# A bias line stored earlier in the load queue, x loaded first, squares ahead of the line copy, and nine products of zeros ahead of the first square sums

## The chip, the cores and the metric

The kernel runs on one core of one Trainium2 chip. The metric is the time of one execution on the device in microseconds (us), as the median of repeated runs. The core has five engines that run side by side: TensorE (PE in the profile, its weight loads PEld), VectorE (DVE), ScalarE (ACT), GpSimd (POOL) and SyncE (SP), which here issues almost all DMA transfers. They are ordered by semaphores alone.

## The reference, cut to what matters

The reference is two transformer-like blocks on 256 tokens of width 1024. What the change touches is the very beginning of the first block:

```python
# first layer: pool mixer, then a gated feed-forward
x = x + pool_mixer(rmsnorm(x, norm_mixer[0]), pool_w[0], pool_scale[0])
x = x + swiglu(rmsnorm(x, norm_ffn[0]), w_gate_up[0], w_down[0])

def rmsnorm(x, g):
    return x * rsqrt(mean(x * x) + EPS) * g
# pool_mixer: window sums of 2, 4, 8, 16 tokens / counts - h, then a 256x256 product per group
# attention, much later: scores + rel_bias[bucket(distance)] per head
# second block: mod = silu(c) @ ada_w + ada_b   (a 1024 x 6144 matrix)
```

After it come attention with a relative bias, a second feed-forward, and a second block with attention, an RWKV branch and 64 experts.

## The kernel before

All work is written out by hand, one program per engine. Tokens lie along the free dimension, features along the partitions, in eight chunks of 128; `x`, `h` and `sq` are 128 x 8 x 256. Weights stream through a ring of 11 slots of 1536 KB each; SP issues the loads in a fixed order, and what it issues is worked off in that order.

SP's order at the start (L505 to L527) is: the 33 x 512 selector, the 33 x 24 relative bias `relw`, the vectors `vecs`, `x`, the inverse counts, two slots of the modulation matrix (`load_ada(0)`, `load_ada(1)`), the pool weights, `load_ada(2)`, `load_ada(3)`, the first feed-forward slot (`load(0)`, a `ws` transfer), then a wait for `line_copied`, the constants `con`, the store `bias_line<-scr`, and the further `ws` slots. The store writes one 512-wide line per head (24 heads) to DRAM, each repeated 32 times, so that the attention can later read it back in shifted form (`bias1`, read by POOL some hundred microseconds later).

The line itself is one small product: PE multiplies `relw` with the selector (L799), ACT copies the result out of PSUM into `line_sb` (L1426, `line_copied`). ACT then squares x (`norm_squares(0)`, L1366, four instructions), PE sums the squares with a matrix of ones (`norm_sum(0)`, L693), and ACT takes the root into `rt` (L1369). DVE makes the normalized `hp` (L1753, L1755), the window sums (L1870 to L1873) and four groups of pool inputs (L1878, L1879), each group signalled by `pool_d`. PE meanwhile does the first three quarters of the modulation product (`modulation(0, 0, 6)`, L792), which wants the `ada` slots 0, 1 and 2, and stands ahead of the pool products (L811) in its program; the last quarter and `norm_sum(1)` come behind them.

ACT waits for all four `pool_d` and for slot 0 of `ws`, and copies that slot's gate and up part into `gu_hi` (L1376). DVE's program at this place is the function `first_start`:

```python
                pool_residual(0)
                pool_residual(1)
                split()                      # slot_lo <- slot 0 - gu_hi, L1759: waits for ACT's gu_hi
                dve.wait_ge(line_stored, 16)
                h_lo_pair(0)                 # L1768
                pool_residual(2)             # L1885
                h_lo_pair(1)
                pool_residual(3)
                h_lo_pair(2)
                h_lo_pair(3)
                add_modulation(0)
```

`line_stored` must be waited for before the feed-forward because `act_hi`, which DVE writes in it, lies over `line_sb`. The residuals 2 and 3 behind it release ACT's last two pairs of squares, these the last products of `norm_sum(1)`, and these the feed-forward's four clearing products (L699) and its long row of products in three parts (L715 to L717).

Of the kernel before, what the change touches and what calls it, by code (L numbers as in the profile page):

```python
# [12 lines left out]
ACT = mybir.ActivationFunctionType  # L13
# [4 lines left out]
P = 128  # L18
T = 256
# [18 lines left out]
SHIFTS = 32  # L38
# [110 lines left out]
def build(nc, xT, vec, consts, selector, inv_count, pool_w, ws, ada, rel, lora, router, router_bias, experts, final_row, out):  # L149
# [4 lines left out]
    with ExitStack() as ctx:  # L154
# [347 lines left out]

        @block.sync
        def _(sp):
            sp.dma_start(sel_sb[0:BUCKETS + 1, :], selector).then_inc(sel_loaded, 16)  # L505
            sp.dma_start(relw[:], rel).then_inc(sel_loaded, 16)
            sp.dma_start(vecs[:], vec).then_inc(vec_loaded, 16)
            sp.dma_start(x[:], xT).then_inc(x_loaded, 16)
            sp.dma_start(icnt, inv_count).then_inc(pool_loaded, 16)

            def load(n):
# [2 lines left out]
            def load_ada(a):  # L514
                p = ADA_PLACE[a]
                sp.dma_start(ring[:, p * SLOT:(p + 1) * SLOT], ada[a]).then_inc(landed[p], 16)

            load_ada(0)
            load_ada(1)
            sp.dma_start(poolw, pool_w).then_inc(pool_loaded, 16)  # L520
            load_ada(2)
            load_ada(3)
            load(0)
            sp.wait_ge(line_copied, 1)
            heads = HEADS_1 + HEADS_2
            sp.dma_start(con[:], consts).then_inc(const_loaded, 16)
            sp.dma_start(bias_line, line_sb[0:heads, :].unsqueeze(1).broadcast_to([heads, SHIFTS, 2 * T])).then_inc(line_stored, 16)  # L527

            def load_after(n, signal, value):
                sp.wait_ge(signal, value)  # L530
# [153 lines left out]
        def _(pe):  # L684
# [3 lines left out]
            def norm_sum(k, bank=B[6], weights=lambda c: ones[:]):  # L688

                for g in range(4):  # L690
                    pe.wait_ge(sq_ready, SQ_BASE[k] + g + 1)
                    for c in (2 * g, 2 * g + 1):
                        mm = nc.tensor.matmul(bank[:, 0:T], weights(c), sq[:, c, :], start=(c == 0), stop=(c == KC - 1))  # L693
                mm.then_inc(ss_ready, 1)
# [86 lines left out]
            def modulation(g, c0, c1):  # L781
# [5 lines left out]
                for c in range(c0, c1):  # L787
# [6 lines left out]
                    if (c + 1) * chunk // SLOT > first:  # L794
                        mm.then_inc(ada_used, 1)

            pe.wait_ge(ones_ready, 1)
            pe.wait_ge(sel_loaded, 32)
            nc.tensor.matmul(B[7][0:HEADS_1 + HEADS_2, :], relw[:], sel_sb[0:BUCKETS + 1, :], start=True, stop=True).then_inc(pe_step, 1)  # L799


            norm_sum(0)
            pe.wait_ge(csil_ready, 2)
            pe.wait_ge(line_copied, 1)
            modulation(0, 0, 6)
# [541 lines left out]
        def _(act):  # L1347
            def load_table(func):

                nc.scalar.activation(small[:, 60:61], eps, func)  # L1350
# [68 lines left out]
                return exponentials, outputs, turned_weights  # L1419

            act.wait_ge(ones_ready, 1)
            act.wait_ge(vec_loaded, 16)
            nc.scalar.activation(csig, vecs[:, VEC["c"][0]:VEC["c"][1]], ACT.Sigmoid).then_inc(csil_ready, 1)
            load_table(ACT.Sqrt)
            act.wait_ge(pe_step, 1)
            nc.scalar.activation(line_sb[0:HEADS_1 + HEADS_2, :], B[7][0:HEADS_1 + HEADS_2, :], ACT.Copy).then_inc(line_copied, 1)  # L1426
            norm_squares(0)

            act.wait_ge(pool_d, 4)
            ffn_start(S_FFN1)  # L1430
# [311 lines left out]
        def _(dve):  # L1742
# [129 lines left out]
            then(nc.vector.tensor_tensor(pw_b[:, 4:, 7:W], pw_c[:, 4:, 7:W], pw_c[:, 4:, 3:W - 4], ALU.add))  # L1872
            then(nc.vector.tensor_tensor(pw_c[:, 6:, 15:W], pw_b[:, 6:, 15:W], pw_b[:, 6:, 7:W - 8], ALU.add))  # L1873
            dve.wait_ge(pool_loaded, 32)
            for g in range(4):
                win = (pw_b, pw_c)[g % 2][:, 2 * g:2 * g + 2, PAD:]
                hg = h[:, 2 * g:2 * g + 2, :]
                then(nc.vector.tensor_tensor(hg, win, icnt[:, g:g + 1, :].broadcast_to([P, 2, T]), ALU.mult))  # L1878
                nc.vector.tensor_tensor(hg, hg, hp[:, 2 * g:2 * g + 2, PAD:], ALU.subtract).then_inc(pool_d, 1)  # L1879
# [576 lines left out]
```

## Time and profile before

| | |
|---|---|
| three runs | 1401.15, 1398.17, 1400.96 us, median 1400.96 |
| the profiled execution | 1400.87 us, its span 1399.2 us |
| PE busy | 1330.1 us, 95% of the span |
| DVE, ACT, POOL busy | 678.1, 510.9, 197.9 us |
| mean granted TensorE clock | 0.986 |
| chain that ended last | PE 82%, DVE 8%, ACT 3%, DMA 3% |

The span runs from the first instruction to the last. The table says that PE works nearly all the time; what is left to gain without taking work from PE lies where PE waits, and the change is at the start of the program.

### The profile page before, as it was taken

To read this page: it belongs to the slowest core of one execution; us is meant where nothing else is said; L and a number is where in the kernel's file an instruction comes from. 1 tells how busy PE (TensorE), PEld (TensorE's weight loads), DVE (VectorE), ACT (ScalarE), POOL (GpSimd) and SP (SyncE) were. 2 spreads that over 40 slices of the span, in tenths; PEclk is the share of its full clock that TensorE was granted. 3 is DMA by queue.
4 is the path that set the end of the run, shared out by engine and by line. 5 is a ranking of instruction groups with operands and counts; after the bars stand their busy time and mean duration, and the time that the engine had idled before them with its cause. 6 is when DMAs were issued, how large, how long until landed. Compare 5 with 4: busy or idle time off the path is not lost.

```text
span 1399.2 us, 24627 instructions
## 1 busy us (share of the span) xinstructions
PE 1330.1 (95%) x10580; PEld 1013.9 (72%) x10580; DVE 678.1 (48%) x1075; ACT 510.9 (37%) x829; POOL 197.9 (14%) x96
## 2 busy tenths in 40 slices
PE   5899999999999999999997889999999999999997
PEld 3899999988899999799895789744444444444433
DVE  6665665666666665788985443511121112212113
ACT  2433433556533333467454442222222222222212
POOL 0000000000000000376781663000000000000002
PEclk9999999999999999999999999999999999999999
DMA  9965455745455336452316035349999999999994
GB/s 370 408 271 185 176 185 217 302 130 215 168 182 188 148 123 231 193 215 96 138 46 271 3 118 225 122 193 423 423 426 426 423 428 426 422 428 424 422 426 174
DMA packets 37507, 363.43 MB, mean 260 GB/s; under 512 B 5027, under 2 KB 6179, under 8 KB 8740
## 3 DMA queue, kind: packets, MB, share of 16 engines
q1 hardware_dynamic: 36692, 359.56, 63.8%
q0 software_dynamic: 720, 2.46, 0.9%
q8 instruction: 77, 1.26, 0.4%
q14 instruction: 18, 0.15, 0.0%
HBM read 359.32 MB, written 2.69 MB: 259 GB/s over the span
## 4 chain that ended last, share of the span: by engine, by line
PE 82%; DVE 8%; ACT 3%; DMA 3%; POOL 2%; issue 1%; SPq 0%; DVEq 0%; POOLq 0%; ACTq 0%
PE banks L1289 16%; PE banks L715 13%; PE banks L717 13%; PE banks L716 13%; PE banks L1314 8%; PE banks L1240 4%; PE banks L1249 4%; DMA bias_line<-scr 2%; POOL slot_lo L627 2%; PE banks L693 1%; PE banks L704 1%; PE banks L1255 1%; DMA scr<-bias_line 1%; PE banks L1063 1%; DVE ring L2077 1%
## 5 line engine op out<-in xcount | busy, mean ns | idle before, releaser
L715 PE MATMUL banks<-h_hi,gu_hi 128*128 128x256 f32 x704 | 199.5, 283 | 0.0
L717 PE MATMUL banks<-h_hi,slot_lo 128*128 128x256 f32 x704 | 199.2, 283 | 0.0
L716 PE MATMUL banks<-h_lo,gu_hi 128*128 128x256 f32 x704 | 199.2, 283 | 0.0
L717 PE MATMUL banks<-slot_lo,slot_lo 128*128 128x256 f32 x480 | 136.3, 284 | 0.0
L715 PEld LDWEIGHTS banks<-h_hi,gu_hi 128*128 128x128 f32 x704 | 135.2, 192 | 0.7 <-DVE slot_lo L1759 0.5
L716 PEld LDWEIGHTS banks<-h_lo,gu_hi 128*128 128x128 f32 x704 | 135.2, 192 | 0.0
L717 PEld LDWEIGHTS banks<-h_hi,slot_lo 128*128 128x128 f32 x704 | 135.2, 192 | 0.0
L2313 DVE TENSOR_TENSOR out_lo<-banks,out_hi 128x512 fp32r<-128x512 f32 x62 | 42.9, 692 | 185.0 <-ACT out_hi L1701 185.0
L1314 PE MATMUL banks<-ring,scr 128*64 128x512 f32 x512 | 116.9, 598 | 1.9 <-ACT scr L1695 1.9
L1289 PE MATMUL banks<-ring,scr 128*64 128x512 f32 x512 | 112.6, 592 | 0.0
L1289 PE MATMUL banks<-ring 128*64 128x512 f32 x512 | 112.6, 592 | 0.0
L1759 DVE TENSOR_TENSOR slot_lo<-ring,gu_hi 128x2048 fp32r<-128x2048 f32 x44 | 100.7, 2292 | 14.4 <-ACT gu_hi L1380 14.0
L1392 ACT ACTIVATE scr<-scr 128x256 f32<-128x256 f32 x44 | 18.4, 418 | 236.1 <-DVE scr L1788 236.1
L2291 DVE TENSOR_TENSOR scr<-banks,scr 128x256 f32<-128x256 f32 x32 | 13.6, 425 | 184.1 <-ACT scr L1688 184.1
L715 PE MATMUL banks<-act_hi,down_hi 128*128 128x256 f32 x352 | 99.9, 284 | 2.6 <-DVE slot_lo L1759 2.6
L716 PE MATMUL banks<-act_lo,down_hi 128*128 128x256 f32 x352 | 99.6, 283 | 0.0
L717 PE MATMUL banks<-act_hi,slot_lo 128*128 128x256 f32 x352 | 99.6, 283 | 0.0
L627 POOL TENSOR_TENSOR slot_lo<-ring,win_hi 128x1024 fp32r<-128x1024 f32 x20 | 48.4, 2426 | 314.4 <-ACT win_hi L1508 314.4
L717 PEld LDWEIGHTS banks<-slot_lo,slot_lo 128*128 128x128 f32 x480 | 92.2, 192 | 0.0
L1289 PEld LDWEIGHTS banks<-ring,scr 128*64 128x64 f32 x512 | 36.7, 137 | 73.3 <-issue 73.3
L1289 PEld LDWEIGHTS banks<-ring 128*64 128x64 f32 x512 | 36.8, 137 | 73.0 <-issue 73.0
L1688 ACT ACTIVATE scr<-banks 128x256 f32<-128x256 f32 x32 | 12.3, 385 | 208.5 <-PE banks L1289 208.5
(420 smaller groups left out, 2985.3 us busy)
## 6 DMA issues: line engine op xcount, KB each, us to landing
ring<-experts SPq DMA_DIRECT2D x64, 2048.0 KB, 10.9
ring<-ws SPq DMA_DIRECT2D x77, 1536.0 KB, 7.2
ring<-experts SPq DMA_DIRECT2D x64, 1024.0 KB, 11.0
ring<-ada SPq DMA_DIRECT2D x16, 1536.0 KB, 7.0
ring<-experts SPq DMA_DIRECT2D x1, 3072.0 KB, 10.1
scr<-bias_line POOLq DMA_DIRECT2D x4, 512.0 KB, 8.0
bias_line<-scr SPq DMA_DIRECT2D x1, 1536.0 KB
x<-xT SPq DMA_DIRECT2D x1, 1024.0 KB, 5.3
```

The costliest lines, as they stand in the source:

```text
L627: nc.gpsimd.tensor_tensor(dst, src, hi.bitcast(F32), ALU.subtract).then_inc(win_w_lo, 1)
L693: mm = nc.tensor.matmul(bank[:, 0:T], weights(c), sq[:, c, :], start=(c == 0), stop=(c == KC - 1))
L715: nc.tensor.matmul(out, hi, move_hi, start=start, stop=False, skip_group_check=True)
L716: nc.tensor.matmul(out, hi, move_lo, start=False, stop=False, skip_group_check=True)
L717: return nc.tensor.matmul(out, lo, move_hi, start=False, stop=stop, skip_group_check=True)
L1240: mm = nc.tensor.matmul(bank, tok[:, tb, step * P:(step + 1) * P], pick[buf][:, tb, :], start=(n == 0 and tb == 0), stop=(n == 1 and tb == ...
L1249: mm = nc.tensor.matmul(B[2 * tb + half], spread[k % 2][:, tb * P:(tb + 1) * P], part[:, half * 512:(half + 1) * 512], start=False, stop=F ...
L1289: mm = nc.tensor.matmul(B[4][CAP * j:CAP * (j + 1), :], gathered_h[o][:, c, at:at + CAP], unit(u)[:, c * 512:(c + 1) * 512], start=(c == 0 ...
L1314: mm = nc.tensor.matmul(B[6 + half][CAP * j:CAP * (j + 1), :], act_pt[:, f, CAP * j:CAP * (j + 1)], unit(u)[:, lo:lo + 512], start=(f == 0 ...
L1392: nc.scalar.activation(gated[:, s % 2, :], gated[:, s % 2, :], ACT.Silu).then_inc(sig_ready, 1)
L1759: nc.vector.tensor_tensor(slot_lo[PLACE[base + s]][:, lo:to], slot(base + s)[:, lo:to], hi.bitcast(F32), ALU.subtract).then_inc(signal, 1)
L2313: ins = nc.vector.tensor_tensor(out_lo[part], B[6 + half], out_hi[part].bitcast(F32), ALU.subtract)
```

## The change

Five edits, all in the first part of the program. SP issues `x` and `vecs` ahead of the selector and `relw`; the store of the bias line stands, with its wait, right behind the pool weights, ahead of `load_ada(2)`, `load_ada(3)` and `load(0)`. PE runs nine products of zeros (128 x 512, bf16) as soon as `ones_ready` is there, then `norm_sum(0)`, and the product of the bias line only behind that. ACT loads the sigmoid table by a small instruction before the vectors are there, and copies the line only behind `norm_squares(0)`. DVE waits for that product (`pe_step`) before it writes `h`, since `h` lies over the selector.

```diff
@@ block.sync
+            sp.dma_start(x[:], xT).then_inc(x_loaded, 16)
+            sp.dma_start(vecs[:], vec).then_inc(vec_loaded, 16)
             sp.dma_start(sel_sb[0:BUCKETS + 1, :], selector).then_inc(sel_loaded, 16)
             sp.dma_start(relw[:], rel).then_inc(sel_loaded, 16)
-            sp.dma_start(vecs[:], vec).then_inc(vec_loaded, 16)
-            sp.dma_start(x[:], xT).then_inc(x_loaded, 16)
             sp.dma_start(icnt, inv_count).then_inc(pool_loaded, 16)
...
             sp.dma_start(poolw, pool_w).then_inc(pool_loaded, 16)
+            sp.wait_ge(line_copied, 1)
+            heads = HEADS_1 + HEADS_2
+            sp.dma_start(bias_line, line_sb[0:heads, :].unsqueeze(1).broadcast_to([heads, SHIFTS, 2 * T])).then_inc(line_stored, 16)
             load_ada(2)
             load_ada(3)
             load(0)
-            sp.wait_ge(line_copied, 1)
-            heads = HEADS_1 + HEADS_2
             sp.dma_start(con[:], consts).then_inc(const_loaded, 16)
-            sp.dma_start(bias_line, line_sb[0:heads, :].unsqueeze(1).broadcast_to([heads, SHIFTS, 2 * T])).then_inc(line_stored, 16)
@@ block.tensor
+            def keep_clock(n):
+
+                for _ in range(n):
+                    nc.tensor.matmul(B[5], zeros[:, 0:P], zeros[:], start=True, stop=True, skip_group_check=True)
+
             pe.wait_ge(ones_ready, 1)
+            keep_clock(9)
+            norm_sum(0)
             pe.wait_ge(sel_loaded, 32)
             nc.tensor.matmul(B[7][0:HEADS_1 + HEADS_2, :], relw[:], sel_sb[0:BUCKETS + 1, :], start=True, stop=True).then_inc(pe_step, 1)
-
-
-            norm_sum(0)
@@ block.scalar
             act.wait_ge(ones_ready, 1)
+            nc.scalar.activation(small[:, 61:62], eps, ACT.Sigmoid)
             act.wait_ge(vec_loaded, 16)
             nc.scalar.activation(csig, vecs[:, VEC["c"][0]:VEC["c"][1]], ACT.Sigmoid).then_inc(csil_ready, 1)
             load_table(ACT.Sqrt)
+            norm_squares(0)
             act.wait_ge(pe_step, 1)
             nc.scalar.activation(line_sb[0:HEADS_1 + HEADS_2, :], B[7][0:HEADS_1 + HEADS_2, :], ACT.Copy).then_inc(line_copied, 1)
-            norm_squares(0)
@@ block.vector
             dve.wait_ge(pool_loaded, 32)
+            dve.wait_ge(pe_step, 1)
             for g in range(4):
```

On SP the two orders stand against each other like this, from the inverse counts on (one piece of the difference; the slots `ring<-ada` and `ring<-ws` are 1536 KB each):

```order
 L509 DMA scr<-inv_count 128x1024
 L516 DMA ring<-ada 128x3072 x2
 L520 DMA scr<-pool_w 128x2048
+L523 DMA bias_line<-scr 768x1x512
 L516 DMA ring<-ada 128x3072 x2
 L512 DMA ring<-ws 128x3072
-L526 DMA con<-consts 128x1505
-L527 DMA bias_line<-scr 768x1x512
+L527 DMA con<-consts 128x1505
 L512 DMA ring<-ws 128x3072 x25
```

The store moved ahead of two `ada` slots and the first `ws` slot, which together are three slots of 1536 KB.

On ACT the order before, from the sigmoid's table to the first copy of a weight slot:

```order
L1423 ACT_TABLE_LOAD
L1423 ACTIVATE small<-vecs 128x8
L1350 ACT_TABLE_LOAD
L1350 ACTIVATE small<-small 128x1
L1426 ACTIVATE scr<-banks 24x512
L1366 ACTIVATE scr<-x 128x512 x4
L1369 ACTIVATE rt<-banks,small 128x256
L1376 ACTIVATE gu_hi_51<-ring 128x2048
```

And of the change (its line numbers are four to six higher):

```order
L1426 ACT_TABLE_LOAD
L1426 ACTIVATE small<-small 128x1
L1428 ACTIVATE small<-vecs 128x8
L1354 ACT_TABLE_LOAD
L1354 ACTIVATE small<-small 128x1
L1370 ACTIVATE scr<-x 128x512 x4
L1373 ACTIVATE rt<-banks,small 128x256
L1432 ACTIVATE scr<-banks 24x512
L1380 ACTIVATE gu_hi_51<-ring 128x2048
```

The copy of the line (`scr<-banks 24x512`) moved from ahead of the squares to behind the root, and one small instruction with the sigmoid's table stands in front.

On PE, the start of the program (one piece of the difference; the store of the line hangs on L799, now L806, by way of ACT's copy):

```order
-L799 MATMUL banks<-scr,relw 24x512
+L800 MATMUL banks<-zeros 128x512 x9
 L693 MATMUL banks<-scr,ones 128x256 x8
+L806 MATMUL banks<-scr,relw 24x512
 L792 MATMUL banks<-ring,small 32x384 x24
-L811 MATMUL banks<-scr 128x256 x16
+L815 MATMUL banks<-scr 128x256 x16
```

The product of the line moved behind the square sums; the modulation (L792) still stands ahead of the pool products (L811, now L815), whose own place is the same.

## Rows read from the trace of the kernel before

**Rows 1.** The page: span, chain that ended last; the windows view after 46.1 us.

```profile
span 1399.2 us, 24627 instructions
...
PE 82%; DVE 8%; ACT 3%; DMA 3%; POOL 2%; issue 1%; SPq 0%; DVEq 0%; POOLq 0%; ACTq 0%
...
46.10:1399.20 1353.10, 1302.52 (x10448) 997.59 (x10446) 650.85 (x1027) 496.84 (x805) 197.66 (x92) 0.99 0.64 256
```

**Rows 2.** Timeline of DVE: start, duration, line, shape, idle time before and releaser.

```profile
32.78 2.29 DVE L1759 TENSOR_TENSOR slot_lo<-ring,gu_hi 128x2048 fp32r<-128x2048 f32 x1 [0.41 <-ACT gu_hi L1376]
38.75 0.88 DVE L1768 SCALAR_TENSOR_TENSOR h_lo<-x,vecs,h_hi 128x256 fp32r<-128x256 f32 x2 [3.67 <-DMA bias_line<-scr]
39.55 0.87 DVE L1885 SCALAR_TENSOR_TENSOR x<-banks,vecs,x 128x256 f32<-128x256 f32 x2
...
41.12 0.87 DVE L1885 SCALAR_TENSOR_TENSOR x<-banks,vecs,x 128x256 f32<-128x256 f32 x2
```

**Rows 3.** Timeline of PE, 3 to 47 us.

```profile
3.13 1.87 PE L799 MATMUL banks<-scr,relw 33*24 33x512 f32 x2 [3.13 <-DMA relw<-rel]
8.14 5.29 PE L693 MATMUL banks<-scr,ones 128*128 128x256 f32 x16 [3.15 <-ACT scr L1366]
...
22.29 2.79 PE L792 MATMUL banks<-ring,small 128*32 128x384 f32 x16 [4.68 <-DMA ring<-ada]
26.97 7.14 PE L811 MATMUL banks<-scr 128*128 128x256 f32 x32 [1.89 <-DVE scr L1879]
34.05 1.50 PE L792 MATMUL banks<-ring,small 128*32 128x384 f32 x16
...
41.93 3.67 PE L693 MATMUL banks<-scr,ones 128*128 128x256 f32 x8 [4.46 <-ACT scr L1366]
45.40 1.08 PE L699 MATMUL banks<-zeros 128*128 128x512 bf16 x4
46.12 0.47 PE L715 MATMUL banks<-h_hi,gu_hi 128*128 128x256 f32 x1
46.43 0.28 PE L716 MATMUL banks<-h_lo,gu_hi 128*128 128x256 f32 x1
```

**Rows 4.** Timeline of ACT, 5 to 43 us.

```profile
5.26 1.28 ACT L1350 ACT_TABLE_LOAD   x1
...
6.67 0.57 ACT L1426 ACTIVATE scr<-banks 24x512 f32<-24x512 f32 x1
7.46 2.19 ACT L1366 ACTIVATE scr<-x 128x512 f32<-128x512 f32 x4 [0.22 <-DMA x<-xT]
...
30.84 1.91 ACT L1376 ACTIVATE gu_hi<-ring 128x2048 fp32r<-128x2048 f32 x1 [16.89 <-DVE scr L1879]
...
42.84 0.61 ACT L1366 ACTIVATE scr<-x 128x512 f32<-128x512 f32 x1
```

**Rows 5.** Timeline of SP, the DMA issues.

```profile
0.88 0.44 SPq L505 DMA_DIRECT2D scr<-selector  x1
...
2.13 0.43 SPq L508 DMA_DIRECT2D x<-xT  x1
...
4.33 0.45 SPq L520 DMA_DIRECT2D scr<-pool_w  x1
4.82 1.08 SPq L516 DMA_DIRECT2D ring<-ada  x2
5.94 0.49 SPq L512 DMA_DIRECT2D ring<-ws  x1
7.26 0.33 SPq L526 DMA_DIRECT2D con<-consts  x1
7.63 0.93 SPq L527 DMA_DIRECT2D bias_line<-scr  x1
```

**Rows 6.** Issues in narrow windows: KB each, us from issue to landing.

```profile
x<-xT SPq DMA_DIRECT2D x1, 1024.0 KB, 5.3
scr<-pool_w SPq DMA_DIRECT2D x1, 1024.0 KB, 14.2
ring<-ada SPq DMA_DIRECT2D x1, 1536.0 KB, 17.4
ring<-ws SPq DMA_DIRECT2D x1, 1536.0 KB, 23.7
con<-consts SPq DMA_DIRECT2D x1, 752.5 KB, 24.6
```

**Rows 7.** Timeline and issue row of the first `ws` behind the store.

```profile
8.62 19.31 SPq L512 DMA_DIRECT2D ring<-ws  x1
...
ring<-ws SPq DMA_DIRECT2D x1, 1536.0 KB, 35.9
```

**Rows 8.** Windows: stretch, length, busy of PE, PEld, DVE, ACT, POOL, clock, DMA share, GB/s.

```profile
7.00:28.00 21.00, 12.04 (x69) 6.48 (x70) 13.74 (x17) 2.90 (x6) 0.00 (x0) 0.92 1.02 431
31.00:35.00 4.00, 4.00 (x27) 2.82 (x29) 3.59 (x5) 4.00 (x8) 0.00 (x0) 1.00 1.00 354
35.00:39.00 4.00, 2.47 (x16) 1.44 (x8) 0.33 (x2) 0.48 (x1) 0.00 (x0) 1.00 0.96 295
...
42.46:45.87 3.41, 3.41 (x10) 2.23 (x9) 2.40 (x6) 1.22 (x4) 0.00 (x0) 0.56 0.99 422
```

## The prediction, made before the changed kernel was run

> **What bounds the kernel now.** I read the page first. PE is busy for 1302.5 of the 1353.1 us behind 46.1 us, and the chain that ended last is 82% PE [rows 1]. No edit touches anything behind 46 us, so the change is worth what it does to the moment at which PE's long row of three-part products starts. Before, its steady row begins at 46.43 us [rows 3]. Then I read the timelines back from there. The row waits for the four clearing products of L699, these for `norm_sum(1)`, which ends at 41.93 + 3.67 = 45.60, this for ACT's last square, 42.84 + 0.61 = 43.45 [rows 3, 4], and this for the last pool residual on DVE, 41.12 + 0.87 = 41.99 [rows 2]. DVE runs its chain without a hole from 38.75 on; there it had sat idle for 3.67 us, until `bias_line<-scr` had landed [rows 2]. So the store's landing sets the start now. The reader is to see one more thing: what stands just behind that wait. DVE's split of slot 0 (32.78 + 2.29 = 35.07) hangs on ACT's copy, which ended at 30.84 + 1.91 = 32.75, and this began 1.2 us after the slot's landing at 5.94 + 23.7 = 29.64 [rows 2, 4, 5, 6]. The pool products began at 26.97, 1.9 us after the modulation products, which waited for the third `ada` slot, landed at 4.82 + 17.4 = 22.22 [rows 3, 5, 6].
>
> **The queue is what the change really moves.** From 7 to 28 us it moves 431 GB/s at a DMA share of 1.02 [rows 8]: it is full, and whatever is put ahead of a transfer delays it. The store now stands ahead of two `ada` slots and the first `ws` slot. Its price S in the queue isn't shown directly; I bound it. From below: its 1536 KB (1.57 MB) at 431 GB/s are 3.65 us. From above: the constants landed at 7.26 + 24.6 = 31.86 and the `ws` slot right behind the store at 8.62 + 35.9 = 44.52, 12.66 us for the store and that slot; with 3.65 for the slot, 9.0 are the store's [rows 5 to 8]. In between lies its own landing, 7.63 + 31.09 = 38.72 by the end of DVE's idle time at 38.75, 6.9 us after the constants. While it ran, the queue moved only 354 and 295 GB/s at a share of 1.00 and 0.96 [rows 8], so it fills the DMA engines without bringing their bytes. I take 9.0, since what matters here is the landing of slots behind the store, and the row of such a slot is the nearest.
>
> The Trainium skill (DMA: Bandwidth & Descriptors, section on the anatomy of one DMA, measured for transfers that GpSimd issues) has about 2 us fixed plus bytes at 436 GB/s. By that rule the store would take 3.6 us of the queue, and the change would come out as the first rival below; the trace's 295 to 354 GB/s speak against it.
>
> **Head of the queue.** `x` is issued first, at 0.88 in place of 2.13 [rows 5]. That moves `x` from 2.13 + 5.3 = 7.43 to about 6.2, and everything behind by 0 to 1.25 us; I take 1.0, as the small transfers that stood ahead still cost their packets.
>
> **The store's start.** ACT needs `vecs` (now behind `x`), the small sigmoid, the table of the root (1.28) and then squares for 2.19 us [rows 4]: it starts them at 7.5 to 8, as before, for before they began at 7.46. The square sums take 5.29 us as now, 0.33 us a record, or, at the rate of the pool products (7.14 / 32 = 0.22 us a record [rows 3]), 3.6. So they end at 11.8 to 13.5; then 1.87 for the line's product, 0.57 for the copy [rows 3, 4], and 0.93 for the issue [rows 5]: the store is in the queue between 15 and 17 us. The pool weights ahead of it land at 4.33 + 14.2 = 18.5, less 1.0. So the queue doesn't run dry, or by half a microsecond at most.
>
> **The sum.** The first `ws` slot lands at 29.64 - 1.0 + 9.0 = 37.6, ACT's copy ends at 39.6, DVE's split at 41.9 (2.29), and `h_lo_pair(0)` starts there in place of 38.75: 3.1 us later, though the wait for the store is gone. Is something else later? The third `ada` slot lands at 22.2 - 1 + 9 = 30.2, the modulation takes 2.8 at the low clock, and the pool products run from 33.0. PE has then sat idle for long, and some of them run at 1.2 GHz; two groups end at 36.6 to 38.6, three by 40.4, four by 43.0, and residuals 0 and 1 are done on DVE by 39.6, 2 and 3 find their groups ready. So the `ws` slot decides. From 41.9 DVE's chain takes its 3.24 us (38.75 to 41.99) and ACT's last square ends at 41.9 + 3.24 + 1.46 = 46.6.
>
> Behind it something is given back. Before, PE had sat idle for 4.46 us ahead of the last four products of the sum, and ran them and the clearing at a granted clock of 0.56, 2.98 us from the last square to the steady row (43.45 to 46.43) [rows 3, 8]. Now pool products, modulation (1.50) and the first half of the sum fill PE until about 44, so the clock should be at 2.4 GHz: two products are four records, 0.9 us, and the clearing 0.9. That is 1.8, 1.2 us less. The steady row starts at 48.4 in place of 46.43: 3.1 - 1.2 = +1.9 us.
>
> **Edits at nothing.** The nine products of zeros and the squares ahead of the line's copy can bring the root forward by up to 1.7 us, and with it `hp` and the pool inputs. PE will wait for the third `ada` slot until 30 while DVE has the first pool input at about 26 (PE waited 1.89 us for it, until 26.97 [rows 3]); so 4 to 7 us of cover hide whatever comes of them. Without that cover they were worth up to 1.7 us. The early sigmoid's table hides in the wait for `vecs`. DVE's new wait for `pe_step` stands ahead of the first pool input, which PE had at 26.97; the product is done by 15.4 (13.5 + 1.87). The constants land at 31.86 - 1.0 + 9.0 = 39.9; DVE wants them behind its chain, after 45.1. The further `ws` slots have the same bytes ahead of them as before; the next one is due at 43.5 to 44.5 and ACT wants it behind the root of the second norm, after 47.
>
> **The time.** The sum is made against the profiled execution, 1400.87 us with a span of 1399.2, all but the median of the three runs (1400.96). 1400.9 + 1.9 = 1402.8.
>
> **The rivals.**
>
> First, the store costs only its bytes, 3.65 us. The trace's low rates beside it speak against; for it speaks that another place has other neighbours. Then the slots land at 24.9 (`ada`) and 32.3 (`ws`). ACT ends at 34.2, DVE's split at 36.5, 2.25 us earlier than 38.75; with the 1.2 us of the clock 3.4 us are gained: 1397.5. Chance 0.10. The shift of the start is S - 7.1 us by the sum above, so it passes -2.8 us (0.2%) when S is under 4.3.
>
> Second, slower by more than 0.2%: the same mechanism with the head of the queue not moved (+1.0), the queue dry for half a microsecond before the store, or PE's clock not back for the last sums (+1.2): 1403.8 with the first alone, 1405.5 with all three. It decides from 0.9 us above my sum, so the first or the last alone is enough. What speaks for it is that PE idles longer ahead of the modulation than the 4.68 us of before, as the slot comes 8 us later. Chance 0.30.
>
> Third, S near the store's own landing, 6.9: slot at 35.5, `h_lo_pair(0)` at 39.8, +1.1 - 1.2: no change, 1400.8. It lies with my forecast within 0.2%; the two together 0.60. That the nine products don't raise the clock changes no number here.
>
> **How the numbers follow.** About 0.2% (2.8 us) is what a measurement of this kernel can tell from no change. Forecast and third rival, from -0.1 to +1.9 us and their surroundings, hold 0.60 within it, the first rival 0.10 faster, the second 0.30 slower. The range takes in S from 4.8 to 9.0 us (1400.9 - 2.3 = 1398.6) and of the second rival's additions all but the last half microsecond: 1398.6 to 1405.0.
>
> **What would show it.** In the changed kernel's timeline: DVE no longer waits for `bias_line`; ACT's copy into `gu_hi` waits for `ring<-ws` until about 37.6 and not for DVE; PE's modulation waits for `ring<-ada` until about 30; the store lands before 27; the last four records of `norm_sum(1)` take 0.9 us; PE's steady row starts near 48.4. The prediction is wrong if the `ws` slot lands before 34 us, if PE's pool products end after the split, or if something behind 50 us moves by itself.

## The result and the profile after

The changed kernel takes 1408.05 us (median of 6 runs, 1404.73 to 1409.61), the kernel before 1400.5 beside it (6 runs). The ratio is 1.0047, 95% interval 1.0028 to 1.0066: slower by about half a per cent, above the predicted range of 1398.6 to 1405.0. The profiled execution took 1409.61 us.

The page's head and its busy times, for the changed kernel:

```profile
span 1407.8 us, 24641 instructions
...
PE 1333.9 (95%) x10586; PEld 1015.6 (72%) x10589; DVE 678.1 (48%) x1075; ACT 511.0 (36%) x830; POOL 198.1 (14%) x96
```

DVE and ACT have worked as long as before; the span is 8.6 us longer, PE's busy time 3.8. I read the front in the order of the prediction. SP's timeline (start, duration) of the changed kernel:

```profile
0.88 0.40 SPq L505 DMA_DIRECT2D x<-xT  x1
...
4.13 0.43 SPq L520 DMA_DIRECT2D scr<-pool_w  x1
16.50 0.94 SPq L523 DMA_DIRECT2D bias_line<-scr  x1
17.49 2.62 SPq L516 DMA_DIRECT2D ring<-ada  x2
20.15 2.25 SPq L512 DMA_DIRECT2D ring<-ws  x1
```

Its issue rows in narrow windows (KB, us from issue to landing):

```profile
scr<-pool_w SPq DMA_DIRECT2D x1, 1024.0 KB, 13.6
...
ring<-ada SPq DMA_DIRECT2D x1, 1536.0 KB, 16.2
...
ring<-ws SPq DMA_DIRECT2D x1, 1536.0 KB, 21.6
```

The store was issued at 16.50 us, within the forecast 15 to 17. But the pool weights had landed by 4.13 + 13.6 = 17.7, the third `ada` slot came at 17.49 + 16.2 = 33.7 (before 22.2, [rows 5, 6]) and the first `ws` slot at 20.15 + 21.6 = 41.75 (before 29.64). The windows view of the changed kernel (columns as in [rows 8]) shows the queue there:

```profile
17.00:18.30 1.30, 1.30 (x24) 0.63 (x20) 1.26 (x4) 0.00 (x0) 0.00 (x0) 1.00 0.14 33
19.00:22.00 3.00, 0.36 (x7) 0.00 (x0) 2.96 (x5) 0.00 (x0) 0.00 (x0) 1.00 0.92 221
22.00:25.00 3.00, 0.00 (x0) 0.00 (x0) 2.93 (x3) 0.00 (x0) 0.00 (x0) 0.81 0.98 265
25.00:28.00 3.00, 0.00 (x0) 0.00 (x0) 2.90 (x4) 0.00 (x0) 0.00 (x0) 0.50 0.99 263
...
48.20:51.60 3.40, 2.00 (x7) 1.44 (x8) 3.18 (x9) 2.33 (x5) 0.00 (x0) 0.94 1.02 430
51.60:55.00 3.40, 3.18 (x12) 2.12 (x13) 2.46 (x3) 2.53 (x4) 0.00 (x0) 0.56 0.98 416
```

From 17.0 to 18.3 us the queue is nearly dry, 33 GB/s, and while the store runs, until 28.3, it moves 221 to 265 GB/s, the share of what is queued behind it included. Before, it moved 354 and 295 beside the store [rows 8]. What follows, on ACT, DVE and PE of the changed kernel (timelines):

```profile
8.11 2.17 ACT L1370 ACTIVATE scr<-x 128x512 f32<-128x512 f32 x4
...
15.89 0.59 ACT L1432 ACTIVATE scr<-banks 24x512 f32<-24x512 f32 x1 [0.49 <-PE banks L806]
41.83 1.91 ACT L1380 ACTIVATE gu_hi<-ring 128x2048 fp32r<-128x2048 f32 x1 [25.35 <-DMA ring<-ws]
...
50.07 0.61 ACT L1370 ACTIVATE scr<-x 128x512 f32<-128x512 f32 x1
```

```profile
43.77 2.29 DVE L1764 TENSOR_TENSOR slot_lo<-ring,gu_hi 128x2048 fp32r<-128x2048 f32 x1 [2.16 <-ACT gu_hi L1380]
45.98 0.88 DVE L1773 SCALAR_TENSOR_TENSOR h_lo<-x,vecs,h_hi 128x256 fp32r<-128x256 f32 x2
```

```profile
1.76 4.02 PE L800 MATMUL banks<-zeros 128*128 128x512 bf16 x9 [1.76 <-DVE scr L1866]
8.78 6.11 PE L693 MATMUL banks<-scr,ones 128*128 128x256 f32 x16 [3.00 <-ACT scr L1370]
...
33.73 2.79 PE L792 MATMUL banks<-ring,small 128*32 128x384 f32 x16 [14.37 <-DMA ring<-ada]
36.45 7.69 PE L815 MATMUL banks<-scr 128*128 128x256 f32 x32
...
49.16 1.13 PE L693 MATMUL banks<-scr,ones 128*128 128x256 f32 x4 [1.50 <-ACT scr L1370]
50.73 1.67 PE L693 MATMUL banks<-scr,ones 128*128 128x256 f32 x4 [0.45 <-ACT scr L1370]
52.62 1.49 PE L699 MATMUL banks<-zeros 128*128 128x512 bf16 x3 [0.22 <-issue]
...
54.55 0.31 PE L715 MATMUL banks<-h_hi,gu_hi 128*128 128x256 f32 x1
54.70 0.28 PE L716 MATMUL banks<-h_lo,gu_hi 128*128 128x256 f32 x1
```

DVE's wait for `bias_line` (3.67 us, [rows 2]) is gone, and ACT waits 25.35 us for the `ws` slot in its place. `h_lo_pair(0)` starts at 45.98 instead of 38.75. Behind it a second loss shows. The granted clock, 1.00 (2.4 GHz) from 48.20 to 51.2 us, was at half (1.2 GHz) from there to 54.6, after PE had waited 1.50 and 0.45 us for squares; the last four square sums and the clearing products ran into that.

To compare kernels I use the second product of the steady row. Before it starts at 46.43 [rows 3]. In the changed kernel the fifth is the first that takes 0.28 us, at 54.70; three products of 0.12 us earlier is 54.3, the same row shifted by 7.9 us. The shift is of one execution of each kernel; ACT's table loads further on, at 235 to 1384 us of the kernel before, come 7.9 to 9.0 us later in the changed one, so in these two executions the loss is the front's.

### The profile page after: what moved, and what is told of

Its sections match the earlier page's. It is cut to its first block, busy times and chain, and to the rows that moved or that the text cites. A ratio compares the mean times of both kernels' runs of the same rounds, so it can differ in the third digit from the quotient of the medians.

```text
span 1407.8 us, 24641 instructions
## 1 busy us (share of the span) xinstructions
PE 1333.9 (95%) x10586; PEld 1015.6 (72%) x10589; DVE 678.1 (48%) x1075; ACT 511.0 (36%) x830; POOL 198.1 (14%) x96
## 4 chain that ended last, share of the span: by engine, by line
PE 82%; DVE 8%; ACT 3%; DMA 3%; POOL 2%; issue 1%; SPq 0%; DVEq 0%; POOLq 0%; ACTq 0%
PE banks L1293 16%; PE banks L715 13%; PE banks L717 13%; PE banks L716 13%; PE banks L1318 8%; PE banks L1244 4%; PE banks L1253 4%; POOL slot_lo L627 2%; DMA ring<-ws 2%; PE banks L693 1%; PE banks L704 1%; PE banks L1259 1%; DMA scr<-bias_line 1%; PE banks L1067 1%; DVE ring L2083 1%
## 5 line engine op out<-in xcount | busy, mean ns | idle before, releaser
L1764 DVE TENSOR_TENSOR slot_lo<-ring,gu_hi 128x2048 fp32r<-128x2048 f32 x44 | 100.7, 2292 | 16.2 <-ACT gu_hi L1384 14.0
L2297 DVE TENSOR_TENSOR scr<-banks,scr 128x256 f32<-128x256 f32 x32 | 13.6, 424 | 184.1 <-ACT scr L1693 184.1
L1693 ACT ACTIVATE scr<-banks 128x256 f32<-128x256 f32 x32 | 12.3, 385 | 208.5 <-PE banks L1293 208.5
```

What stands on the lines that cost most here:

```text
L1764: nc.vector.tensor_tensor(slot_lo[PLACE[base + s]][:, lo:to], slot(base + s)[:, lo:to], hi.bitcast(F32), ALU.subtract).then_inc(signal, 1)
```

## The experiments

Each edit is against the kernel before or the changed one, as named. "Row" is the start of the second product of the steady row. The kernel before had medians of 1399.2 to 1399.6 us (28 to 33 runs) beside the repeated experiments, 1395.91 and 1400.09 beside the kernels that were timed once. The row is read in one execution, and scatters: the same kernel, with DVE's wait moved, had it at 43.26 and at 44.49 in two. "Slot" is the landing of the third `ada` slot or of the first `ws` slot, and the store's own time runs from the first to the last of its pieces in the view of the DMA queue, in steps of 0.2 us.

**Which edit costs the time.** The changed kernel with the store back at its old place:

```diff
-            sp.wait_ge(line_copied, 1)
-            sp.dma_start(bias_line, ...)
             load_ada(2)
             load_ada(3)
             load(0)
+            sp.wait_ge(line_copied, 1)
             sp.dma_start(con[:], consts)
+            sp.dma_start(bias_line, ...)
```

> The changed kernel with the store of the bias line (and its wait) put back behind the constants; all else of the change stays. Theory 1, the store's place in the queue is the whole loss: ws slot 0 lands near 29 us again, the wait of DVE for bias_line comes back, the steady row of PE starts at 45.5 to 47, the time is 1399.5 to 1402. Rival, the late line copy and the products of zeros cost by themselves: the line is copied at 16.5 us here too, but nothing hangs on it until the constants; if the time stays above 1404 the theory falls. For the store's price: it is issued near 17 us with some 12 us of transfers ahead of it; if its pace depends on how long its descriptors have stood ready, it takes 7 us as before, not 11.

1400.08 us, ratio 1.0001 [0.9989, 1.0012], row 44.93 (a little earlier than expected); DVE waits for `bias_line` again, 0.93 us. Of the whole loss nothing is left: the store's place costs it. The windows and the PE row of this kernel also tell of the zeros:

```profile
6.50:9.90 3.40, 1.27 (x5) 1.15 (x6) 0.17 (x1) 3.37 (x7) 0.00 (x0) 0.95 1.07 449
9.90:13.40 3.50, 3.50 (x10) 2.73 (x10) 0.00 (x0) 0.24 (x1) 0.00 (x0) 0.56 0.98 414
```

```profile
8.63 5.41 PE L693 MATMUL banks<-scr,ones 128*128 128x256 f32 x16 [2.85 <-ACT scr L1370]
```

Behind the zeros PE waited 2.85 us for the squares; the granted clock reads half while the sums ran, and they took 5.41 us, as long as without zeros (5.29, [rows 3]). The reading of 1.00 from the program's start is not to be trusted: the nine zeros took 447 ns each under it (4.02 us, above), and 18 such products took 226 ns each under the same reading in a kernel below that has zeros in PE's waits (4.06 us). The same kernel without the zeros:

```diff
-            keep_clock(9)
```

> Like a_store_back, without the nine products of zeros. Theory: the zeros never raised the clock for the first square sums (they took 6.1 us with them), so without them the sums take 5.3 to 6.1 us and the time is that of a_store_back within 1 us. Rival, the zeros cost or help: the steady row differs by more than 1 us from that of a_store_back.

1396.53 us, 0.9983 [0.9972, 0.9995], sums 5.57 us, row 45.23. At the front the zeros give nothing that shows: the rows differ by 0.3 us, by which the store had landed earlier (DVE goes on at 38.22 with them, at 38.52 without). The front is as expected, the time isn't: the medians are 3.5 us apart where 1 was allowed. In the two profiled executions that difference arises behind 280 us, where the clock falls at other moments in each. The two pairs with other zeros further down show the same sign, 0.9992 with them against 0.9975 and 0.9991 against 0.9974. So zeros at the front seem to cost some 0.17% of the whole kernel, though how isn't shown.

The kernel before, with the store alone moved (the line is copied early, so the store is issued early):

> The kernel before with nothing but the store moved ahead of the third ada slot; the line is copied at 7.3 us, so the queue is full for 10 us when the store is issued. Theory 1a, the store is slow only when the queue has run dry at its issue: it takes 7 us of the queue, ws slot 0 lands at 37 to 38.6, steady row at 48 to 49.5, time 1402 to 1404. Rival 1b, the store is slow in this place whatever stands ahead (10 to 11 us): ws slot 0 lands at 41 or later, steady row at 52 or later, time 1406 to 1409.

1402.15 us, 1.0034 [1.0018, 1.0051]. SP's, PE's, ACT's and DVE's timelines of this kernel:

```profile
7.23 0.93 SPq L523 DMA_DIRECT2D bias_line<-scr  x1
```

```profile
30.32 2.79 PE L792 MATMUL banks<-ring,small 128*32 128x384 f32 x16 [12.29 <-DMA ring<-ada]
...
46.63 1.13 PE L693 MATMUL banks<-scr,ones 128*128 128x256 f32 x4 [0.45 <-ACT scr L1366]
...
48.58 0.28 PE L716 MATMUL banks<-h_lo,gu_hi 128*128 128x256 f32 x1
```

```profile
37.73 1.91 ACT L1376 ACTIVATE gu_hi<-ring 128x2048 fp32r<-128x2048 f32 x1 [22.04 <-DMA ring<-ws]
```

```profile
41.88 0.88 DVE L1768 SCALAR_TENSOR_TENSOR h_lo<-x,vecs,h_hi 128x256 fp32r<-128x256 f32 x2
```

These are the prediction's own numbers: slot 37.7 (37.6 forecast), `h_lo_pair(0)` 41.88 (41.9), row 48.58 (48.4). In part that is luck: here `x` isn't first, so nothing is gained at the head, and the store's price is 8.1 and not 9.0; the sum had 9.0 - 1.0. What it confirms is the chain from the slot on. In this kernel the store had 11 us of transfers ahead of it and ran for 7.4 us.

**Late issue.** The same kernel with product and copy of the line behind squares and sums, as in the change, without zeros and with the selector first:

```diff
+            norm_sum(0)
             pe.wait_ge(sel_loaded, 32)
             nc.tensor.matmul(B[7]...relw...)
-            norm_sum(0)
...
+            norm_squares(0)
             act.wait_ge(pe_step, 1)
             nc.scalar.activation(line_sb...)
-            norm_squares(0)
```

> The kernel before with the store moved as in b_store_only, and with the product and the copy of the line behind the square sums, as in the change; no products of zeros, the selector first in the queue as before. Theory D, the store's extra price in the changed kernel comes from its late issue into a queue that has nearly run dry: it is issued at 15.5 to 17, takes 10 us where b_store_only's took 7.4, ws slot 0 lands at 40.5 to 42, steady row at 52 to 54.5, time 1406 to 1409. Rival, the products of zeros or the early x did it: then this one stays near b_store_only, steady row at 48 to 49.5, time 1401 to 1404.

1405.31 us, 1.0049 [1.0033, 1.0066]; issued 15.15, store about 9.3 us, slots 31.9 and 39.35, row 50.20: between the two forecasts, nearer to the theory in the store's time and the kernel's. There the pool weights landed at 18.7, so the queue had not run dry. The reverse, the changed kernel with product and copy early again:

> The changed kernel with one thing taken back: the line's product ahead of the square sums (behind the zeros) and its copy ahead of the squares. Theory D: the line is copied at 9 to 10 us, the store issued then with 8 us of transfers ahead of it and takes 7.4 us, slot 0 lands at 36.5 to 38, steady row at 47.5 to 49, time 1401 to 1404. Rival (zeros or the early x cost by themselves): steady row still at 52 or later, time 1406 or more.

1405.0 us, 1.0045 [1.003, 1.0061]; issued 9.74, store 7.5 us. ACT's row for the `ws` slot:

```profile
40.05 1.91 ACT L1380 ACTIVATE gu_hi<-ring 128x2048 fp32r<-128x2048 f32 x1 [23.94 <-DMA ring<-ws]
```

Half a miss: the `ada` slot came at 31.3 but the `ws` slot only at 40.0, and the clock fell at the end as in the changed kernel (last eight records 3.65 us), row 51.95. The store itself was as fast as forecast; why the slot came 2 to 3 us later isn't shown. So an early issue makes the store itself quick, but this kernel isn't faster for it than the one with the late issue (1405.31), and its slot came later than that one's: the store's own time isn't all that its place costs.

One slot ahead of the store in place of none:

```diff
+            load_ada(2)
             sp.wait_ge(line_copied, 1)
             sp.dma_start(bias_line, ...)
-            load_ada(2)
             load_ada(3)
```

> The changed kernel with the store behind the third ada slot in place of ahead of it, its issue still after the late copy, near 16.5 us, so that some 4 us of transfers are in the queue at its issue. Theory D1, what is slow is making the store's descriptors, a rate of its own of 768 in 10 to 11 us from the issue on: the store begins near 21 and ends near 27 to 28.5, hence 6 to 7.5 us in the queue. Rival D2, the slow store is a matter of the time or of its neighbours and not of its issue: it takes 10 us again and ends at 31. In both the third ada slot lands at 21 to 22 and the modulation no longer waits 14 us. Slot 0 lands at 36 (D1) or 38.5 and more (D2); steady row at 47 to 48.5 or 50 and more.

1404.82 us, 1.0051 [1.0032, 1.0069]; issued 16.24 as in the change, store 7.7 us, `ws` slot 37.9, row 48.74. ACT's and PE's rows:

```profile
37.90 1.91 ACT L1380 ACTIVATE gu_hi<-ring 128x2048 fp32r<-128x2048 f32 x1 [21.68 <-DMA ring<-ws]
```

```profile
45.22 1.13 PE L693 MATMUL banks<-scr,ones 128*128 128x256 f32 x4 [1.50 <-ACT scr L1370]
46.80 1.13 PE L693 MATMUL banks<-scr,ones 128*128 128x256 f32 x4 [0.45 <-ACT scr L1370]
```

So it isn't the hour of the issue that makes the store slow but how little stands ahead of it. The row is 2.3 us later than before, the time 0.5%, some 6 to 7 us: in the repeated runs the row alone doesn't give the time. Two kernels that were timed once say it from the other side. The store alone moved, but issued only when the pool weights had landed:

```diff
             sp.wait_ge(line_copied, 1)
+            sp.wait_ge(pool_loaded, 32)
```

> b_store_only (line copied early, at 7.3 us) with one more wait on SP ahead of the store, for the pool weights, so that the store is issued at 18.5 into an empty queue. Theory D, an issue just before the store's turn makes it slow: it takes 9 to 10.5 us. Rival, the slow store came from the late square sums or copy on PE and ACT at that time: it takes 7.4 us as in b_store_only.

1406.19 us against 1395.91; store 10.3 us, slots 36.0 and 43.45, row 54.30. And the changed kernel in which SP waits behind the store until it has landed:

```diff
             sp.dma_start(bias_line, ...)
+            sp.wait_ge(line_stored, 16)
             load_ada(2)
```

> The changed kernel with SP waiting for line_stored behind the store, so that nothing else is issued while it runs. If the transfers issued right behind it slow a late store, it takes 7.4 us here; if a late issue alone does, it takes 10. Everything behind lands later, so the steady row comes at 56 us or later in both.

1410.44 us. The windows view, with nothing but the store in the queue:

```profile
19.00:22.00 3.00, 0.57 (x8) 0.00 (x0) 2.97 (x6) 0.00 (x0) 0.00 (x0) 1.00 0.74 160
22.00:25.00 3.00, 0.00 (x0) 0.00 (x0) 2.97 (x2) 0.00 (x0) 0.00 (x0) 0.92 0.73 157
```

The store takes 10.3 us at 157 to 160 GB/s without any neighbour, at a DMA share of 0.73, about that of 12 engines of 16. The transfers behind it don't slow it.

**What makes it slow: pieces, source lines or engines.** Half of each line at the store's new place, the other half behind the constants, DVE's wait behind `add_modulation(0)`:

```diff
-            sp.dma_start(bias_line, line_sb[0:heads, :]...)
+            sp.dma_start(bias_line[:, :, 0:T], line_sb[0:heads, 0:T]...)
```

> The changed kernel with the store cut in two: the first 256 columns of every line at the store's new place, the other 256 behind the constants, each 768 pieces of 1 KB; DVE's wait, now for both, moved as in c_wait_late. Theory P1, a late store goes by its number of pieces from the issue on: 768 pieces end 11 to 12.5 us after the issue at 16.5 although the bytes are halved, and ws slot 0 lands at 40 or later. Rival P2, it goes by bytes: the first half ends 6 to 8 us after its issue, slot 0 lands at 36 to 38. The steady row is at 50 to 54 under P1, 46 to 49 under P2.

1401.76 us, 1.0021 [1.0009, 1.0033], `ws` slot 37.14, row 49.16; the half took 5.2 us with as many pieces: the price goes by bytes (0.79 MB in 5.2 us are 151 GB/s). Then, timed once each, on the kernel with the store alone moved, the same bytes out of 128 partitions of `ada` slot 0, in pieces of 2 KB and of 12 KB (what is stored isn't the reference's bias, and SP waits for the store before it loads over that slot):

```diff
-            sp.dma_start(bias_line, line_sb[0:heads, :]...)
+            sp.wait_ge(landed[ADA_PLACE[0]], 16)
+            sp.dma_start(bias_line.rearrange(...), ada_slot)
```

> b_store_only with another source: in place of the line, 24 partitions each read 32 times, the store takes the 128 partitions of ada slot 0, in 768 pieces of 2 KB to the same DRAM tensor (the attention's bias is then not the reference's). Its price in the queue is 7.4 us with the line. If the few source partitions make it slow it takes 3.7 to 4.5 us here; if 2 KB pieces or writes to DRAM do, 6.5 to 7.5.

> As r_wide_2kb, but each partition's 12 KB go to one place in DRAM, 128 pieces in all (the bias is not the reference's here either). If writes to DRAM are slow by their bytes it takes 6.5 to 7.5 us, if only small pieces are slow 3.7 to 4.5.

1396.78 and 1397.48 us beside 1395.91. From 19 to 22 us, 2 KB first, then 12 KB (windows view, of each kernel its own):

```profile
19.00:22.00 3.00, 0.00 (x0) 0.00 (x0) 2.97 (x3) 0.00 (x0) 0.00 (x0) 0.60 1.05 394
```

```profile
19.00:22.00 3.00, 0.00 (x0) 0.00 (x0) 2.97 (x2) 0.00 (x0) 0.00 (x0) 0.94 1.02 434
```

With all partitions as source the third `ada` slot lands 5.5 us (2 KB) and 4.4 us (12 KB) later than before, against 8.1 for the line. Both expectations for 2 KB (3.7 to 4.5, or 6.5 to 7.5) missed it. By one execution each, the 2 KB pieces cost 1.1 us over those of 12 KB, and the narrow source 2.6 more. Last, 16 lines stored 48 times in place of 24 stored 32 times, same bytes and pieces, to tell the number of engines from that of source lines (not the reference's bias), in the kernel with the store alone moved and in the changed one:

```diff
-            line_sb[0:heads, :].unsqueeze(1).broadcast_to([heads, SHIFTS, 2 * T])
+            line_sb[0:16, :].unsqueeze(1).broadcast_to([16, 48, 2 * T])
```

> The kernel before with the store alone moved, as the run with the store alone, but the store takes 16 partitions of the line 48 times in place of 24 partitions 32 times: the same 1536 KB in the same 768 pieces of 2 KB, and what is stored isn't the reference's bias. With 24 lines the trace shows 12 pieces in flight at a time (DMA share 0.73 where nothing else moved). T1, the store uses only 12 of the 16 DMA engines because 24 lines share out over 12: with 16 lines 16 pieces are in flight, the store takes 7.4 x 12 / 16 = 5.6 us, the third ada slot lands near 28.5 (30.3 with 24 lines) and the first ws slot near 35.9 (37.7). T2, few source partitions are the limit: 16 are fewer than 24, so it takes 7.4 us or up to 11, and the slots land at 30.3 and 37.7 or later.

> The changed kernel with the same store of 16 partitions 48 times (what is stored isn't the reference's bias), issued late at 16.5 us. T1a, each piece of a late store takes 151 ns on its engine whatever the number of engines: with 16 in flight the store takes 10.2 x 12 / 16 = 7.7 us, third ada slot 31.2 (33.7 with 24 lines), first ws slot 39.2 (41.75), 49 us or a little less for the second product of the steady row. T1b, a late store is bound by something all engines share at about 157 GB/s: pieces take 200 ns, the store still 10 us, the slots land at 33.7 and 41.7. T2 as T1b or later.

1406.97 and 1409.67 us beside 1400.09. The windows of the first, then of the second:

```profile
22.00:25.00 3.00, 0.00 (x0) 0.00 (x0) 2.93 (x3) 0.00 (x0) 0.00 (x0) 0.50 0.93 102
```

```profile
22.00:25.00 3.00, 0.00 (x0) 0.00 (x0) 2.93 (x3) 0.00 (x0) 0.00 (x0) 0.57 0.94 104
```

T1 and T1a fall, and T2 holds in its sign only: the late store of 16 lines took 15.4 us. More engines were at work (share 0.93 to 0.94 against 0.73), and yet the rate fell from 157 to about 103 GB/s; the slots came at 36.5 and 44.0, and at 37.6 and 45.0. Per source line that is 157 / 24 = 6.5 and 103 / 16 = 6.4 GB/s: the rate goes with the number of lines that are read. The Trainium skill (SBUF — State Buffer, section "Door 1: The DMA port swizzle") says that four neighbouring partitions share a port, and gives 435 GB/s for the 16 ports: by an estimate from that page 24 lines reach 6 ports, 163 GB/s, 16 lines reach 4, 109 GB/s. The traces agree, with 157 to 160 for 24 lines alone in the queue and 100 to 104 for 16; by that estimate the store alone takes 9.6 us, measured 10.3. Both sources have four lines to a port, so these runs don't tell a limit of the port from one of the line. And the estimate doesn't hold for the 24-line store that has waited in the queue: it took 7.4 us, 213 GB/s on average.

**The stall itself.** The kernel before, with nothing but DVE's wait moved:

```diff
                 split()
-                dve.wait_ge(line_stored, 16)
                 h_lo_pair(0)
...
                 add_modulation(0)
+                dve.wait_ge(line_stored, 16)
```

> The kernel before with only DVE's wait for line_stored moved behind its last step ahead of the feed-forward, where the line's memory is first written. Theory: the 3.67 us of idle time go, nothing else stood behind them; h_lo_pair(0) starts at 35.1, the steady row 3.7 us earlier and up to 1.2 more where the clock stays up, at 41.5 to 42.8: 1396 to 1397.5. Rival: the next slot, landing at 44.5, becomes the wait and half of it is lost: 1398 to 1399.5.

1394.75 us, 0.9975 [0.9963, 0.9986]. In its timelines of DVE and PE

```profile
33.57 0.88 DVE L1885 SCALAR_TENSOR_TENSOR x<-banks,vecs,x 128x256 f32<-128x256 f32 x2 [1.74 <-PE banks L811]
...
36.56 0.87 DVE L1768 SCALAR_TENSOR_TENSOR h_lo<-x,vecs,h_hi 128x256 fp32r<-128x256 f32 x2
```

```profile
27.17 9.82 PE L811 MATMUL banks<-scr 128*128 128x256 f32 x32 [2.69 <-DVE scr L1879]
...
43.26 0.28 PE L716 MATMUL banks<-h_lo,gu_hi 128*128 128x256 f32 x1
```

`h_lo_pair(0)` starts at 36.56, 2.2 us earlier, and the row at 43.26, 3.2 us earlier, where 35.1 and 41.5 to 42.8 were expected; what DVE waits for now are the pool products, 9.82 us long at the low clock (7.14 before). The time is better than the 1396 to 1397.5 expected. Products of zeros in PE's waits ahead of them:

```diff
-            modulation(0, 0, 6)
+            modulation(0, 0, 4)
+            keep_clock(18)
+            modulation(0, 4, 6)
+            keep_clock(6)
```

> c_wait_late (DVE's wait for the store moved behind its last step) with 18 products of zeros on PE in its wait for the third ada slot and 6 ahead of the pool products. In c_wait_late the pool products took 9.82 us for want of clock and PE is busy from there to the feed-forward. Theory: the zeros keep the clock at 2.4 GHz, the pool products take 7.1 to 7.5 us, the steady row starts 1 to 2.5 us before c_wait_late's 43.4, time 1392.5 to 1394. Rival: DVE's and ACT's chain (residuals, squares) is the bound there already and the steady row moves by less than 0.5 us, time as c_wait_late's, 1394 to 1396.

1397.13 us, 0.9992 [0.998, 1.0004], row 42.53: 1392.5 to 1394 were forecast, so this is a miss. Both again, side by side:

> c_wait_late unchanged, timed again on one chip with the next two. If its gain is real, 0.9963 to 0.9986 again (1394 to 1396 where the kernel before has 1399 to 1400), steady row at 43 to 43.7. Rival: the gain of the first timing was luck of the clock behind 50 us; then the ratio's interval touches 0.999.

> h_warm unchanged, on the same chip as c2_wait_late. Its front part was 0.7 us faster than c_wait_late's in the profile and its time 2.4 us slower in another call. If the zeros cost something behind the front part, it is again 1.5 us or more above c2_wait_late; if that was the chip or the clock's later falls, it lies within 1 us of it.

1396.23 us, 0.9974 [0.9965, 0.9983]: the gain of the moved wait holds. With the zeros 1396.88, 0.9991 [0.9979, 1.0002]. The zeros did at the front what was wanted: the windows view from 21 to 30 us, without zeros and with them, and PE's row with them,

```profile
21.00:30.00 9.00, 4.70 (x21) 2.18 (x22) 8.76 (x10) 0.00 (x0) 0.00 (x0) 0.50 1.00 414
```

```profile
21.00:30.00 9.00, 5.75 (x36) 3.23 (x35) 8.76 (x11) 0.00 (x0) 0.00 (x0) 1.00 1.00 412
```

```profile
17.24 4.06 PE L800 MATMUL banks<-zeros 128*128 128x512 bf16 x18
...
27.44 7.14 PE L819 MATMUL banks<-scr 128*128 128x256 f32 x32 [2.55 <-DVE scr L1887]
```

show a granted clock of 1.00 in place of 0.50, pool products of 7.14 us in place of 10.12, and a row at 42.18 in place of 44.49. The whole kernel isn't faster for it. Where the 2.3 us go again stayed open; with the pair above without and with nine zeros this is the third in which the kernel with zeros has the higher ratio. Last, this edit on the changed front (x first, squares first, no zeros, store at its old place):

> d_no_zeros (x and vecs first, squares ahead of the line's copy, store at its old place, no zeros) with DVE's wait moved as in c_wait_late. It prices the early x and the early squares alone, free of the store. Theory: nothing, as ACT's squares start at 7.5 to 8.2 us in both and PE's pool products wait for DVE at 27 to 28; steady row within 0.7 us of c2_wait_late, time within 1 us. Rival: the early x brings its 1.2 us, steady row at 42.3 or earlier.

1396.31 us, 0.9979 [0.9969, 0.9989], row 45.54: the other edits add nothing to the moved wait, and the row is a us later than expected.

## Why the prediction was wrong, step by step

**The mechanism held.** The stall of DVE went away, the `ws` slot took its place, and ACT and DVE followed it by the forecast intervals: slot to `h_lo_pair(0)` 4.2 us (4.3 forecast), from there to the end of ACT's last square 4.7 (4.7). The head came forward by 0.8 (1.0). The issue at 16.50 lay in its range, in part by luck: the square sums ended at 14.89, past the forecast 11.8 to 13.5, and the line's product took 1.04 us and not 1.87. The zeros, the squares and the new waits changed no number in the sum up to the row; that the zeros are worth nothing in the whole time is doubtful, by the three pairs above.

**The step that failed first** is the price of the store: "I take 9.0", together with "the queue doesn't run dry, or by half a microsecond at most". From 29.64 to 41.75 with a head of 0.8 the price was 12.9 us (12.3 at the `ada` slot). Of it 1.0 to 1.3 are the dry queue, 10.2 the store's own time; 1.4 to 1.7 I can't place. Taken the same way this rest is 1.4 us with one slot ahead and 3 us or more with the copy early, both with `x` first, and 0.7 and 0.4 us in the two kernels of the store alone and of the late copy, with the selector first; whether that order does it wasn't tried. My 9.0 came from the rows of a store that had stood in the queue behind several slots, and comes near for such a one: 8.1 in the kernel with the store alone moved, measured at both slots. A store into a dry queue runs at what its 24 lines give, 157 GB/s. That is not between the bounds that I drew, since both came from one place in one queue. The Trainium skill's rule on ports (SBUF — State Buffer, section "Door 1: The DMA port swizzle") would have given 9.6 us for the store alone, an estimate; I had looked at its rule on bytes only. This term, with 0.2 us of the head, makes 4.1 of the 6.0 us by which the row came later than forecast.

**The second step** is "so the clock should be at 2.4 GHz": from the last square to the row 1.8 us were forecast, 54.3 - 50.68 = 3.6 were measured. PE waits for the squares twice in this stretch, 1.50 and 0.45 us, and the granted clock was at half from 51.2 on. With the store alone moved the same step took 48.58 - 46.58 = 2.0. The two waits alone don't decide it: with one slot ahead of the store PE had the same two, 1.50 and 0.45 us, and kept its clock (1.13 us for four records each time), while with the copy early it lost it. What decides stays open, and so whether other executions of the changed kernel lose it too. This term makes 1.9.

**The sum.** 1.9 + 4.1 + 1.9 = 7.9, the shift of the row. The measured medians differ by 1408.05 - 1400.5 = 7.55, and nothing behind 50 us moved by itself beyond the scatter of the two executions. The other kernels warn against leaning on that match of row and median: with the store alone moved the row is 2.1 us later and the time 0.34% (4.8 us), with one slot ahead 2.3 us and 0.51%. The second rival had the place and the sign right, but put its additions at 0.5 for the dry queue and 1.2 for the clock, and had none for a slower store: 1405.5 at most. The range ended at 1405.0, half a microsecond short even of that. The first rival (3.65 us) is far off for this source, and near for the wide source in pieces of 12 KB (4.4 us).

## What to carry to other kernels

A wait on a slow transfer is cheaper cured by moving the wait than by moving the transfer: behind the work that doesn't need it, one line gave 0.25% here, while the store moved ahead cost 0.34% to 0.5%, because three loads came behind it, and the path waits for the last of them. The price of a transfer isn't a number of its own: ask how many partitions it reads from, and whether anything is ahead of it in the queue when it is issued. Here the narrow store issued into a dry queue paid the gap and its full 10 us, and everything behind it paid with it.

## What the runs showed of the hardware

- A store whose source is 24 partitions moves 157 to 160 GB/s with the queue to itself, one of 16 partitions 100 to 104; with one of 128 partitions, queued among others, the queue moves 394 to 434.
- The same 24-line store, issued with 4 us or more of transfers ahead of it, takes 7.4 to 7.8 us in place of 10.2. With the store alone moved, some 150 of its 2 KB pieces end per us at first and about 75 at the end, against 76 to 80 throughout for the one that is alone in the queue. That the engines had read part of it ahead while it waited would fit: in that kernel the pool weights, which stand ahead of the store, landed at 4.67 + 15.1 = 19.8 in place of 18.5. It wasn't tried.
- SP's issues were held up behind the store wherever it stood: by 2.00 and 2.25 us in the changed kernel (the second `ada` slot, within the row at 17.49, and the `ws` slot at 20.15), 5.05 and 3.50 us with the store alone moved, 19.31 us for the `ws` slot behind it in the kernel before [rows 7]. The issues ahead of it took 0.3 to 0.8 us each.
- Nine products of zeros that end 2.85 us before the sums leave them at the low clock (5.41 us, 5.29 without zeros); 18 and 6 of them in PE's waits kept it at 2.4 GHz (pool products 7.14 us against 10.12), without any gain in the whole kernel's time.
